# Taking a norm's factor out of a projection's input and applying it to the results in PSUM

## The reference

```python
xn = rms_norm(x, norm_mix_w)          # x * rsqrt(mean(x*x) + eps) * w
proj = xn @ w_in
hq, hf, hi, hg, fq, fk, fv, ff, ga, gb = split(proj)
a = hgrn2_mixer(hq, hf, hi, hg, lb, hgrn_norm_w)   # 4 heads of 128; ends with rms_norm per head * silu(hg)
b = fox_attention(fq, fk, fv, ff, fox_f_bias)      # 8 heads of 64, causal softmax with forget bias
merged = sigmoid(ga) * (a @ w_branch_hgrn) + sigmoid(gb) * (b @ w_branch_fox)
h = x + merged @ w_out
h = h + peer_ffn(rms_norm(h, norm_ffn_w), ...)     # product-key experts
return rms_norm(h, norm_final_w)
```

## Time and profile before

| | us |
|---|---|
| median of 3 runs (lowest, highest) | 1774.5 (1771.56, 1780.75) |
| profiled execution: its time, its span | 1773.98, 1772.1 |
| TensorE busy | 1718.7 |
| DVE, ACT, POOL busy | 1219.9, 778.3, 782.9 |

### The profile page before, as it was taken

How to read it: one execution, slowest core, us unless ns; L and a number is a source line. 1 busy time by engine, 2 the same in 40 slices (tenths; PEclk the granted TensorE clock), 3 DMA queues, 4 the chain that set the end, 5 groups by cost and what they waited for, 6 DMA issues and landing times.

```text
span 1772.1 us, 25695 instructions
## 1 busy us (share of the span) xinstructions
PE 1718.7 (97%) x9603; PEld 1603.5 (90%) x9603; DVE 1219.9 (69%) x2268; ACT 778.3 (44%) x1367; POOL 782.9 (44%) x488
## 2 busy tenths in 40 slices
PE   6999999999999999999999999998999999999996
PEld 4887887777788999999999999998999999999996
DVE  6445535644432699999899676635888878787884
ACT  4433325543320334347776766633333333333332
POOL 4434432234342678875554567784222222222210
PEclk8999999999999999999999999999999999999998
DMA  6322333255344689997877799998999999999981
GB/s 180 105 72 60 84 107 90 78 164 156 90 137 110 237 296 313 319 304 250 292 252 275 259 342 374 345 402 318 338 351 355 350 347 361 336 366 344 349 294 48
DMA packets 260996, 436.39 MB, mean 246 GB/s; under 512 B 15040, under 2 KB 184256, under 8 KB 259208
## 3 DMA queue, kind: packets, MB, share of 16 engines
q1 hardware_dynamic: 203848, 250.17, 44.0%
q0 software_dynamic: 36864, 134.23, 20.0%
q10 hardware_dynamic: 20160, 50.34, 7.6%
HBM read 373.87 MB, written 60.82 MB: 245 GB/s over the span
## 4 chain that ended last, share of the span: by engine, by line
PE 48%; issue 6%; DVE 5%; POOL 5%; DMA 2%; ACT 1%; SPq 0%; DVEq 0%; POOLq 0%; ACTq 0%
PE bank L223 13%; PE bank L225 13%; PE bank L224 13%; PE x_rows L223 3%; PE x_rows L224 3%; PE x_rows L225 3%; POOL rows L1102 2%; POOL spl_a L218 2%; PE bank L1552 1%; DVE rows L1111 1%; DMA rows<-in_u_rows,expert 1%; DMA raw<-in_u_t 1%; DMA raw<-in_v_tab 1%; DVE hot L1337 1%; DVE lists L1365 0%
## 5 line engine op out<-in xcount | busy, mean ns | idle before, releaser
L218 POOL TENSOR_TENSOR spl_a<-raw,spl_a 128x1024 fp32r<-128x1024 f32 x172 | 415.9, 2420 | 364.3 <-ACT spl_a L214 363.5
L214 ACT ACTIVATE spl_a<-raw 128x1024 fp32r<-128x1024 f32 x296 | 313.0, 1059 | 405.5 <-PE bank L225 280.0
L223 PE MATMUL bank<-act,spl_a 128*128 128x384 f32 (+1 forms) x1216 | 429.4, 353 | 13.1 <-DVE act L541 7.4
L225 PE MATMUL bank<-act,spl_a 128*128 128x384 f32 (+1 forms) x1216 | 419.3, 345 | 0.0
L224 PE MATMUL bank<-act,spl_a 128*128 128x384 f32 (+1 forms) x1216 | 419.1, 345 | 0.0
L1102 POOL DMA_INDIRECT rows<-in_v_tab,expert x128 | 134.8, 1053 | 363.4 <-DVE hot L1478 349.8
L223 PE MATMUL bank<-aws,spl_a 128*128 128x384 f32 x768 | 259.1, 337 | 4.5 <-POOL spl_a L218 4.5
L225 PE MATMUL bank<-aws,spl_a 128*128 128x384 f32 x768 | 258.8, 337 | 0.0
L224 PE MATMUL bank<-aws,spl_a 128*128 128x384 f32 x768 | 258.8, 337 | 0.0
L223 PEld LDWEIGHTS bank<-act,spl_a 128*128 128x128 f32 x1216 | 230.0, 189 | 26.6 <-issue 14.2
L224 PEld LDWEIGHTS bank<-act,spl_a 128*128 128x128 f32 x1216 | 230.0, 189 | 8.1 <-issue 1.4
(11 more groups left out here) (295 smaller groups left out, 2808.4 us busy)
## 6 DMA issues: line engine op xcount, KB each, us to landing
raw<-in_u_t SPq DMA_DIRECT2D x128, 512.0 KB, 4.6
raw<-in_v_tab SPq DMA_DIRECT2D x128, 512.0 KB, 6.8
gelu_ux<-gl ACTq DMA_DIRECT2D x128, 192.0 KB, 4.9
dense_gates<-mixbuf ACTq DMA_DIRECT2D x12, 2048.0 KB, 8.3
mixbuf<-dense_gates SPq DMA_DIRECT2D x32, 768.0 KB, 9.0
mixbuf<-gelu_ux SPq DMA_DIRECT2D x32, 768.0 KB, 12.1
raw<-in_w_in SPq DMA_DIRECT2D x44, 512.0 KB, 3.9
raw<-in_w_q SPq DMA_DIRECT2D x16, 512.0 KB, 4.0
```

The lines of the kernel that those rows point to most:

```text
L214: eng.activation(spl(n, 0, slice(0, W)), raw[:, s, :], ACT.Copy).then_inc(hi_done, 1)
L218: eng.tensor_tensor(spl(n, 1, slice(0, W)), raw[:, n % RAW, :], spl(n, 0, slice(0, W)).bitcast(F32), ALU.subtract).then_inc(lo_done, 1)
L223: nc.tensor.matmul(out, w_hi, x_hi, start=first, stop=False)
L225: return nc.tensor.matmul(out, w_lo, x_hi, start=False, stop=last)
```

## The change

- x is split without the factor: `act` holds x times the norm's weight; ACT makes the high part straight from the loaded x, DVE the low part. Unit 0's low half is made by DVE. Loads are reordered: norm weights, x 0, unit 0, x 1 to 3, unit 1, constants, small vectors, units 2 and 3, masks.
- Squares are summed on DVE and ACT; one matmul with ones after unit 2 gives the mean. The factor `rs` (one row repeated over the partitions) is ready later; four transposes after unit 5 turn it into a column `rs_col` for units 8 to 15.
- Units 0 to 5 go to banks 0 to 5 and wait for no eviction; the mean uses bank 6, the transposes bank 7.
- All units but 8 to 15 leave PSUM by a DVE multiply with `rs`, at the head of DVE's step n behind a wait for unit n. ACT then takes sigmoids from SBUF. Units 8 to 15 leave on ACT with `rs_col` as scale. ff's bias is added by POOL.
- The order of units at the end is 12 merge gates, hg at 37 to 40, four merge gates at 41 to 44. Roots move to step 34, row norms to 35, 36, 38, 39. The gates' landings are waited for in the next block.

```diff
-COLS = COL_HF + COL_HQ + COL_HI + COL_FV + COL_FF + COL_FQ + COL_FK + COL_GATES + COL_HG
+COLS = COL_HF + COL_HQ + COL_HI + COL_FV + COL_FF + COL_FQ + COL_FK + COL_GATES[:12] + COL_HG + COL_GATES[12:]
-ROOT_STEP = 35
-ROW_STEP = [36, 36, 39, 39]
+ROOT_STEP = 34
+ROW_STEP = [35, 36, 38, 39]
+FIRST = 6
...
+            def pbank(n):
+                return bank[n] if n < FIRST else bank[n % 2]
...
             @block.sync
+                sp.dma_start(nrm[:, 0, :], norm_mix).then_inc(nmix_in, 16)
                 for q in range(4):
                     sp.dma_start(late[:, 2 * q:2 * q + 2, :], xv[:, 2 * q:2 * q + 2, :]).then_inc(x_in[q], 16)
                     if q == 0:
-                        sp.dma_start(cst[:, :, :], c_f32).then_inc(consts_in, 16)
+                        load_unit(sp, 0)
+                load_unit(sp, 1)
+                sp.dma_start(cst[:, :, :], c_f32).then_inc(consts_in, 16)
...
             @block.scalar
+                for k in range(KD):
+                    act_e.wait_ge(x_in[k // 2], 16)
+                    act_e.activation(act[:, 0, k, :], late[:, k, :], ACT.Copy, scale=nrm[:, 0, k:k + 1]) \
+                        .then_inc(xw_hi, 1)
+                    if k == 1:
+                        split_hi(act_e, 0)
+                split_hi(act_e, 1)
                 for k in range(0, KD, 2):
-                    act_e.wait_ge(x_in[k // 2], 16)
-                    act_e.activation(kc[:, k, :], late[:, k, :], ACT.Square).then_inc(squares[0], 1)
-                split_hi(act_e, 0)
+                    act_e.activation(kc[:, k, :], late[:, k, :], ACT.Square).then_inc(squares, 1)
+                for n in range(2, LEAD):
+                    split_hi(act_e, n)
                 act_e.wait_ge(mean_ready, 1)
                 act_e.activation(lev[:, 1, :], lev[:, 0, :], ACT.Sqrt).then_inc(root_ready, 1)
-                for k in range(KD):
-                    act_e.wait_ge(xn_ready, k + 1)
-                    act_e.activation(act[:, 0, k, :], late[:, k, :], ACT.Copy).then_inc(xn_hi, 1)
-                for n in range(1, LEAD):
-                    split_hi(act_e, n)
...
                 for n in range(N_IN):
                     split_hi(act_e, n + LEAD)
-                    pr = bank[n % 2]
-                    act_e.wait_ge(unit_used, n + 1)
                     if n < HQ0:
-                        act_e.activation(kk[:, n, :], pr[:, :], ACT.Sigmoid).then_inc(proj_out[n % 2], 1)
+                        act_e.wait_ge(proj_out[n % 2], n // 2 + 1)
+                        act_e.activation(kk[:, n, :], kk[:, n, :], ACT.Sigmoid).then_inc(f_sig, 1)
...
+                    elif HG0 <= n < HG0 + 4:
+                        h = n - HG0
+                        act_e.wait_ge(proj_out[n % 2], n // 2 + 1)
+                        if h >= 2:
+                            act_e.wait_ge(g_done, h - 1)
+                        act_e.activation(lev[:, n % 2, :], kk[:, h, :], ACT.Sigmoid).then_inc(sig_ready, 1)
...
             @block.vector
+                for k in range(KD):
+                    dve.wait_ge(xw_hi, k + 1)
+                    dve.scalar_tensor_tensor(out=act[:, 1, k, :], in0=late[:, k, :], scalar=nrm[:, 0, k:k + 1],
+                                             in1=act[:, 0, k, :].bitcast(F32), op0=ALU.mult, op1=ALU.subtract) \
+                        .then_inc(xw_lo, 1)
+                    if k == 1:
+                        split_lo(dve, 0)
...
-                link(dve.reciprocal(lev[:, 2, :], lev[:, 1, :]))
+                dve.reciprocal(rs[:, :], lev[:, 1, :]).then_inc(rs_ready, 1)
...
                 for n in range(N_IN):
-                    pr = bank[n % 2]
+                    pr = pbank(n)
+                    if not HI0 <= n < FF0:
+                        dve.wait_ge(unit_used, n + 1)
                     if n < HQ0:
-                        dve.wait_ge(proj_out[n % 2], n // 2 + 1)
+                        dve.tensor_tensor(kk[:, n, :], pr[:, :], rs[:, :], ALU.mult).then_inc(proj_out[n % 2], 1)
...
+                    elif gate_no(n) is not None:
+                        g = gate_no(n)
+                        if g >= 2:
+                            dve.wait_ge(spilled[g % 2], 16 * (g // 2))
+                        dve.tensor_tensor(spill[:, g % 2, :], pr[:, :], rs[:, :], ALU.mult) \
+                            .then_inc(proj_out[n % 2], 1)
...
-                    if n >= HG0:
-                        h = n - HG0
+                    if HG0 < n <= HG0 + 4:
+                        h = n - 1 - HG0
                         dve.wait_ge(sig_ready, 4 + h + 1)
...
             @block.tensor
+                    if n == 2:
+                        pe.wait_ge(consts_in, 16)
+                        pe.wait_ge(sum_ready, 1)
+                        nc.tensor.matmul(bank[6][:, :], ones, kc[:, 7, :], start=True, stop=True).then_inc(mean_mm, 1)
+                    if n == FIRST - 1:
+                        pe.wait_ge(rs_ready, 1)
+                        for i in range(NT):
+                            c = slice(i * P, (i + 1) * P)
+                            ins = nc.tensor.transpose(bank[7][:, c], rs[:, c], ident)
+                        ins.then_inc(rs_tr, 1)
```

More of the change, by code:

```diff
@@ L460, in _ @@
                         if n - HQ0 >= 2:
[L461 to L464, removed]
+                            act_e.wait_ge(q_done, n - HQ0 - 1)
+                        act_e.activation(lev[:, n % 2, :], ab[:, n - HQ0, :], ACT.Sigmoid).then_inc(sig_ready, 1)
@@ L465, in _ @@
                     elif n < FF0:
[L466 to L482, removed]
+                        i = n % 4
@@ L530, in _ @@
                 dve.wait_ge(mean_mm, 1)
[L531 removed]
+                dve.tensor_scalar(lev[:, 0, :], bank[6][:, :], 1.0 / D, EPS, ALU.mult, ALU.add) \
                     .then_inc(mean_ready, 1)
                 dve.wait_ge(root_ready, 1)
[L534 to L545 removed]
+                dve.reciprocal(rs[:, :], lev[:, 1, :]).then_inc(rs_ready, 1)
+                dve.wait_ge(rs_ready, 1)
                 dve.wait_ge(lb_exp, 1)
@@ L643, in _ @@
+                    if n == FIRST:
+                        dve.wait_ge(rs_tr, 1)
+                        dve.tensor_copy(rs_col[:, :], bank[7][:, :].rearrange("p (i t) -> p i t", i=NT)[:, :, 0]) \
+                            .then_inc(rs_col_ready, 1)
                     if n == HI0 - 1:
                         dve.wait_ge(pool_zero, 4)
+                        dve.wait_ge(consts_in, 16)
                         for h in range(HH):
@@ L684, in _ @@
                                                           op0=ALU.mult, op1=ALU.mult))
-                    if n >= HG0:
-                        h = n - HG0
+                    if HG0 < n <= HG0 + 4:
+                        h = n - 1 - HG0
                         dve.wait_ge(sig_ready, 4 + h + 1)
-                        link(dve.tensor_tensor(lev[:, n % 2, :], pr[:, :], lev[:, n % 2, :], ALU.mult))
-                        dve.tensor_tensor(ab[:, h, :], ab[:, h, :], lev[:, n % 2, :], ALU.mult) \
-                            .then_inc(proj_out[n % 2], 1)
+                        link(dve.tensor_tensor(lev[:, (n - 1) % 2, :], kk[:, h, :], lev[:, (n - 1) % 2, :], ALU.mult))
+                        dve.tensor_tensor(ab[:, h, :], ab[:, h, :], lev[:, (n - 1) % 2, :], ALU.mult) \
+                            .then_inc(g_done, 1)
             @block.tensor
             def _(pe):
-                pe.wait_ge(consts_in, 16)
-                for k in range(KD):
-                    pe.wait_ge(squares[k % 2], k // 2 + 1)
-                    ins = nc.tensor.matmul(bank[4][:, :], ones, kc[:, k, :], start=k == 0, stop=k == KD - 1)
-                ins.then_inc(mean_mm, 1)
                 def project(n):
                     pe.wait_ge(lo_done, last_step(n) + 1)
-                    if n >= 2:
-                        pe.wait_ge(proj_out[n % 2], n // 2)
-                    out = bank[n % 2][:, :]
+                    if n >= FIRST:
+                        pe.wait_ge(proj_out[n % 2], n // 2 if n >= FIRST + 2 else 1)
+                    out = pbank(n)[:, :]
                     if HI0 <= n < FF0:
```

112 lines of the change are left out of this document (74 added, 38 removed).

## The result

| | before | after |
|---|---|---|
| median of 6 runs each, us (lowest, highest) | 1774.53 (1771.56, 1782.68) | 1790.0 (1787.32, 1795.32) |
| profiled execution: time, span, us | 1773.98, 1772.1 | 1788.77, 1787.0 |

The account below looks back on a forecast made before the run. TensorE, busy 97% of the span, was taken as the bound, so time could come only from its gaps. The terms -12.8 + 8.7 + 2.0 - 0.9 = -3.0 gave a median of 1771.5 us, range 1762 to 1780.

Parts of the forecast that it names:

- Start: Kernel's beginning: statistics leave the path before unit 0, net gain 12.8 us, bounds 8 to 15.
- HGRN steps: Mixer's HGRN steps: evictions move to DVE's queue ahead of the preparation, a loss of 8.7 us.
- eight level steps: HGRN steps with a level's group second: preparation waits behind the eviction, 0.85 us each, 6.8 us in all.
- step 30: HGRN step: six operations behind the eviction cost 1.9 us, 4 if POOL holds one.
- slower rival: HGRN steps: POOL's split holds DVE's preparation in most of ten steps, 1.3 us each, 1784.5 us; chance 0.08.
- Step 19: HGRN step: TensorE's wait falls from 2.7 to 1.6 us, -1.1, bounds -2.7 and +1.0.
- Clock: Granted clock's fall from 160 us on: 1.7 us of work, may vanish; left out of the sum.
- FoX steps: FoX steps: most new evictions lie beside TensorE, but one step loses; +2.0 us in all.
- Step 40: FoX step: ACT's copies come late for TensorE, +2.0 us; 0 if ACT is earlier, 4 if POOL holds a product.
- Boundary: Mixer's end: the last unit needs only one eviction, so 0.9 us are gained, range 0 to 1.3.
- sign of being wrong: TensorE's first matmul after 12 us, step waits under 0.3 or over 1.5 us, or a split wait after unit 6.

Follow-up runs that it names:

- e1: The changed kernel with DVE's preparation of the first HGRN event in steps 16 to 31, and step 21's scan, ahead of the eviction; 1768.95 us, ratio 0.995.
- e10: The changed kernel with POOL's split working on 8 of 1024 columns for the units it splits in steps 17 to 31; 1781.88 us, ratio 1.0033.
- e7: The changed kernel with only step 21's scan of the forget gates put ahead of the unit's wait and eviction; 1786.62 us, ratio 1.0068.
- e6: e1 with step 34's on_mean ahead of that step's eviction and the third head's row norm in step 36 instead of 38; 1766.21 us, ratio 0.992.
- e2: The changed kernel with ACT waiting again for unit n in its steps from 16 on; 1788.65 us, ratio 1.0076.

## Why the prediction was wrong

- **Start, -12.8:** right in kind. TensorE starts at 9.33 us (9.2 forecast), unit 1 at 17.5 (17.25), unit 4 waits 0.90 (0.9). Not forecast: 0.6 at unit 8 for POOL's split. Measured -11.7, and e1 shows that it reaches the end.
- **HGRN steps, +8.7: the step that failed**, as measured +21.4. Its mechanism, the wait behind unit n's eviction, was right, and the eight level steps and step 30 cost 0.9 and 1.8 us in e10, as I had them, but for step 21. That e10's whole is 8.4 is partly luck: step 21 costs 1.1 more than I had, since the scan of 1.21 us stands behind the eviction there, and steps 19 and 20 give back what the kernel before had lost to POOL and to the clock. What failed is the sentence that gave POOL nothing: "by my schedule POOL ends 0.3 us after the unit and DVE arrives 0.9 us after it, 0.6 us apart, which is little". That was one schedule for all steps. ACT makes the high half at another time in each step, and POOL's split of about 2.4 us starts when that is done: in steps 19, 22 and 29 it was running when DVE came. These meetings, with the half clock behind them, are the 13.0 us that e10 takes away. Step 21's own wait of 1.76 us has no POOL operation in it (e10 has the same); moving its scan is worth 3.0 us in all, most of it in step 22 (e7).
- **The slower rival** had this mechanism and 1784.5 us; I gave it 0.08. Its ten times 1.3 us add up to e10's 13.0, by luck, since it was wrong in form: not 1.3 us in each of ten steps, but 2 to 3 us in three or four, and with up to 3.4 us of clock behind the longest.
- **Step 19, -1.1:** wrong sign; the wait rose from 2.7 to 3.49 us. One of POOL's splits does come ahead of the preparation, as I wrote (143.41 to 145.82 us), but the next one, at 147.61, meets it. Without the splits the wait is 1.57 us (e10), the 1.6 that I forecast.
- **Clock:** I left it out of the sum and wrote that the one stretch of before "may vanish". Three stand in its place.
- **FoX steps, +2.0:** measured +5.9. Step 40 cost 3.3 (the wait for ACT's copies 1.4, and 1.7 for the copy behind the eviction: I had the product that POOL holds, 2.73 us here, as a bound, but not the copy that stands behind it), step 34 1.5 for `on_mean` behind an eviction, step 42 1.1. "Most new evictions lie beside TensorE" was the wrong assumption here too: what stood behind them on DVE was not asked.
- **Boundary, -0.9:** right.
- **Range and chances:** 1790.0 us lies above the whole range of 1762 to 1780, and I had given any slowdown 0.06. The sign of being wrong that I had named came: waits of over 1.5 us at the steps.

The rule cited from the Trainium skill, page "SBUF — State Buffer", section "Who interferes with whom", agrees with these traces in both halves. The two-input L602 waits out POOL's split (2.56 us). For the other half the kernel before had no row; e1 has one, the new multiply with one SBUF input, 0.69 us long inside POOL's split:

```profile
168.88 2.36 POOL L226 TENSOR_TENSOR spl_a<-raw,spl_a 128x1024 fp32r<-128x1024 f32 x1 [2.50 <-ACT spl_a L222]
168.91 0.69 DVE L680 TENSOR_TENSOR fk<-bank,rs 128x512 f32<-128x512 f32 x1
...
170.44 1.07 DVE L601 TENSOR_TENSOR lev<-lev,ab 128x256 f32<-128x256 f32 x1
```

L601 behind it, with two SBUF inputs, is held again (1.07 us in place of 0.42). That an operation reads one tile is not enough to spare it: the L588 of before, shown at e10, reads one tile and a column of factors and took 2.26 us beside POOL's split, against 0.28 for the same operation after (L612). The sentence that I cited excepts two-port modes; whether L588 ran in one, no row shows.

## What to carry over

An operation that waits for the end of a long stretch of TensorE should not stand ahead of one that could be done during it: what e1 moves is worth 24.6 us at unit 45, twice what the new start brought. When a preparation loses its cover, price it at its longest duration beside the other engines' work and not at its usual one, and allow for the half clock that stood behind waits of 2.7 us and more in these steps. Idle time of the engine (43.3 us for DVE here) says that there is room, and not that the order lets it be used.

## What I had not expected of the hardware

- In the HGRN steps the half clock followed a wait of TensorE as short as 2.7 us (before) and 2.8 us (after, 0.50 over 3.4 us), and lasted 6.8 us after one of 3.6 us. It didn't follow one of 1.8 us (e7, and e10 throughout). Nor does it follow every longer one: the wait before unit 45 is 3.02 us in the kernel after and in e6, and behind it the clock is 0.50 in the one and 1.00 in the other:

```profile
384.00:386.70 2.70, 2.63 (x6) 2.15 (x7) 2.70 (x5) 2.70 (x6) 0.00 (x0) 0.50 0.95 309
```
```profile
354.90:358.30 3.40, 3.40 (x15) 2.81 (x16) 3.40 (x7) 3.40 (x7) 0.00 (x0) 1.00 0.98 329
```

  What decides it, and what made the third stretch twice as long, no run isolates.
- In the record the DVE operation can start first and still be held to the end of POOL's split: e2's L613 started at 149.35, the split at 149.49, and the DVE operation of 0.28 us took 2.62. It is one case of 0.14 us, and the profile knows POOL's times only roughly.
- Executions differ in the pace of the expert stage at a granted clock of 1.00: 100 us hold 567 to 579 matmuls. Here e1 and e6 (1400 to 1500 us; the first count is TensorE's):

```profile
1400.00:1500.00 100.00, 100.00 (x567) 100.00 (x567) 79.95 (x96) 37.48 (x47) 26.22 (x25) 1.00 0.98 345
```
```profile
1400.00:1500.00 100.00, 100.00 (x579) 100.00 (x578) 81.86 (x98) 38.12 (x48) 26.32 (x25) 1.00 0.99 353
```

That is 2% of such a stretch, and the likely source of the spread of 8 to 14 us among runs of one kernel, though no run isolates its cause. It is why the differences above are read at unit 45.
